# A softmax stage in which every second slot takes a whole output chunk around its transposes, and the slot between them none

## The chip, the cores and the metric

One NeuronCore of a Trainium2 chip runs the whole program. TensorE (PE, and PEld for its weight loads), VectorE (DVE), ScalarE (ACT), GpSimd (POOL) and SyncE (SP, which here only issues DMAs) each run their own list of instructions in order and wait for each other by semaphores. The metric is the time of one execution on the device, in microseconds (us), as the median of several runs.

## The reference

Two layers over a sequence of 2048 tokens with 1024 channels, float32. Layer 0 is windowed attention with a learned sink per head: 16 query heads share 4 key/value heads (4 to each), 64 channels a head, and each block of 128 queries sees its own and the previous block of keys. Layer 1 is a pooling mixer. Around each stand a modulated RMS norm, a gate and a residual.

```python
h = rms_norm(x, norm_g[i]) * (1.0 + scale) + shift
# layer 0
scores = einsum('bnqkgd,bnskd->bnkgqs', qb, kb) * HEAD_DIM ** -0.5     # then masked to the window
m = maximum(max(scores), sink)
p = exp(scores - m)
probs = p / (sum(p) + exp(sink - m))
o = einsum('bnkgqs,bnskd->bnqkgd', probs, vb)
branch = (o * silu(g)) @ w_out
x = x + gate * branch
# layer 1: pooled means over windows of 2, 4, 8, 16, a group projection, silu gate, w_out, gate, residual
```

## The kernel before

Four stages follow one another on all engines: the q, k, v projection (`qkv_stage`), the gate projection (`gate_stage`), attention with its output projection (`attend_stage`), and the whole pooling layer (`pool_stage`). All matmuls are float32 work done as three products of a high and a low part (`PRODUCTS`). The change touches `attend_stage` alone.

The stage runs over 64 units. A unit is one block of 128 queries and one key/value head with its 4 query heads. What one unit needs is spread over several slots of a loop that every engine runs over the same index i. In slot i:

- PE makes the scores of unit i (S: 8 matmuls, `scores`, line 1371), transposes the probabilities of unit i-1 (T: 4 transposes, `p_round`, line 1381), and multiplies the probabilities of unit i-2 by the values (V: 12 matmuls, 6 in the first block, `values`, line 1399).
- ACT copies the previous block's scores out of PSUM (`previous`, line 1183), rounds the gated result of unit i-3 (`z_hi`, line 1207), rounds the transposed probabilities of unit i-1 (`p_hi`, line 1198, which waits for T), takes the four exponentials of unit i (`exps`, line 1191), and the square of a finished output chunk (`square`, line 1217).
- DVE gates the attention output of unit i-3 (`gated`, line 1289, which waits for V of unit i-3), divides the probabilities of unit i-1 (`divide`, lines 1273 and 1275, for which T waits), puts the scores of unit i together and takes their maximum (lines 1265 and 1269), makes the low part of the gated result (line 1296), adds a finished output chunk to x (`residual`, line 1304), and makes the low part of the transposed probabilities (`p_lo`, line 1281).
- POOL masks the four tiles of transposed probabilities of unit i-1 (`mask`, line 1147), and adds the square of a finished chunk to a sum (`add_square`, line 1156).

Each engine's list is fixed by the order of the Python code. So in slot i+1 the division of unit i stands behind the gating of unit i-2, and that waits for V of unit i-2, the last work of PE in slot i. V of unit u also waits for the gating of unit u-1, since both use the same PSUM bank.

The output projection of the stage (O, `output`, line 1415) is 32 chunks: 4 blocks of 512 tokens by 8 blocks of 128 output channels, 24 matmuls of 512 columns each (8 steps of k by 3 products). The last 8 come after the slots. The first 24 are put into slots 19 to 66, two slots for each: chunk c has the slots `first_slot(c)`, which is always odd, and the one after it.

```python
def first_slot(c):
    return LAP * (c // KC + 1) + BEHIND + HALVES * (c % KC)
```

Each of the two slots takes 12 of the 24 matmuls, 6 between S and T and 6 between T and V. Slots 2 to 17 have other work for the same two places (`fold`, line 1432: 6 short matmuls each, with their casts on ACT and DVE). Slot 18 has nothing in either place. Slots 64 to 66 have no S, 65 and 66 no T, and 66 no V. In slots 36 and 52 PE also sums squares (line 1354, 4 matmuls of one column). After slot 66 comes `spread_first` (line 1812), which belongs to the next stage, and then the last 8 chunks with the first norm loads and weight loads of the pooling layer beside them.

The four other engines use a chunk only when both its slots are over (`chunks_ended(i)`, again always an odd slot): SP loads the weights and x of chunk c+3 and stores chunk c, DVE adds the residual, ACT squares it, POOL adds the square.

Of the kernel before, what the change touches and what calls it, by code (L numbers as in the profile page):

```python
# [25 lines left out]
def wait(eng, sem, count):  # L26
    if count > 0:
        eng.wait_ge(sem, count)
# [931 lines left out]
def attend_stage(nc, sem_of, dims, weights, qk, ga, xt_d, sinks_d, wvt, w_group, qt_d, kt_d, vs_d, sg_d, wo_d, wp_d, x1t_d, ident,  # L960
                 gate0, rstd1):

    KC, NB, KV, HEADS, HD, D, GROUPS = (dims[n] for n in ("KC", "NB", "KV", "HEADS", "HD", "D", "GROUPS"))
# [7 lines left out]
    CHUNKS = NSB * KC  # L971
    HALVES = 2
# [11 lines left out]
    def ring(name, n):  # L984
# [13 lines left out]
    keep_cur, sinks, first, half, ones, mq, neg_max, den, rden = (sb[n] for n in (  # L998
        "keep_cur", "sinks", "first", "half", "ones", "mq", "neg_max", "den", "rden"))
# [23 lines left out]
    def first_slot(c):  # L1023
        return LAP * (c // KC + 1) + BEHIND + HALVES * (c % KC)
# [4 lines left out]
    def place(m):  # L1029
        cur, prev = m % 3, (m - 1) % 3  # L1030
        return min(cur, prev), max(cur, prev), 0 if cur < prev else 1
# [315 lines left out]
    def sum_squares(pe, s):  # L1347
        pe.wait_ge(acc_done, (KC - 1) * (s + 1))
        wait(pe, mq_done, s)
        pe.wait_ge(z_done, min(LAP * (s + 2) + 2, UNITS))  # L1350
        if s == NSB - 1:
            pe.wait_ge(x1_done, CHUNKS)
        for t in range(PER):
            last = nc.tensor.matmul(st_columns(s)[:, t:t + 1], acc[:, t * P:(t + 1) * P], ones[:, :], start=True, stop=True)
        last.then_inc(st_done, 1)

    def tensor(pe, spread_first):
        def scores(u):
            m, g = u // KV, u % KV
            low, high, _ = place(m)  # L1360
            if g == 0:
                pe.wait_ge(q_loaded[m % 2], 16 * (m // 2 + 1))
                pe.wait_ge(k_loaded[m % 3], 16 * (m // 3 + 1))
                if m == 0:
                    pe.wait_ge(zero_set, 1)
            wait(pe, cur_done, u - 1)
            if u == 1:
                pe.wait_ge(ga["mod_set"], 2)
            for h in range(GROUP):
                for part in (HI, LO):  # L1370
                    last = nc.tensor.matmul(s_ps[:, u % 2, h, :, :], qt[:, m % 2, GROUP * g + h, :],  # L1371
                                            kt[:, low:high + 1:high - low, g, part, :], start=(part == HI), stop=(part == LO))
            last.then_inc(s_done, 1)

        def p_round(u):
            pe.wait_ge(prob_done, u + 1)
            wait(pe, pl_done, u)
            if u == 0:
                pe.wait_ge(ga["silu_done"], KC * NSB - 1)
            for h in range(GROUP):  # L1380
                last = nc.tensor.transpose(tr[:, h * P:(h + 1) * P], pr[:, u % 2, h, 0:P], ident[:, :])  # L1381
            last.then_inc(ptr_done, 1)

        def values(u):
            m, g = u // KV, u % KV
            if g == 0:
                pe.wait_ge(v_loaded[m % 3], 16 * (m // 3 + 1))
            pe.wait_ge(pt_done, 4 * (u + 1))
            wait(pe, z_done, u)
            if u == 0:  # L1390
                pe.wait_ge(ga["silu_done"], KC * NSB)
            parts = [(m % 3, (CUR_HI, CUR_LO))] + ([((m - 1) % 3, (PREV_HI, PREV_LO))] if m > 0 else [])
            i = 0
            for slot, kinds in parts:
                for v_part, p_part in PRODUCTS:
                    moving = pt[:, u % 2, kinds[p_part], :].rearrange("p (a b t) -> p a b t", a=2, b=2)
                    for parity in (0, 1):
                        v = vs[:, slot, g, v_part, HD - parity * HD:HD - parity * HD + 2 * HD]
                        last = nc.tensor.matmul(o_ps[:, 0:2 * P], v, moving[:, :, parity, :],  # L1399
                                                start=(i == 0), stop=(i == 6 * len(parts) - 1))  # L1400
                        i += 1
            last.then_inc(o_done, 1)

        def output(c, ks):
            s, d = c // KC, c % KC
            if ks[0] == 0:
                pe.wait_ge(w_loaded[c % 3], 16 * (c // 3 + 1))
                wait(pe, x1_done, c - 1)
                if c < 2:
                    pe.wait_ge(fold_out, FOLDS)  # L1410
            if d == 0:
                pe.wait_ge(zlo_done, LAP * (s + 1))
            for k in ks:
                for a, b in PRODUCTS:
                    last = nc.tensor.matmul(y_ps[:, c % 2, :], w[:, c % 3, a, k, :], zt[:, s % 2, b, k, :],  # L1415
                                            start=(k == 0 and (a, b) == PRODUCTS[0]),
                                            stop=(k == KC - 1 and (a, b) == PRODUCTS[-1]))
            if ks[-1] == KC - 1:
                last.then_inc(y_done, 1)

        def fold(u, h):
            f = u // PAIRS
            if h == 0:
                pe.wait_ge(wg_lo, f + 1)
                pe.wait_ge(fold_lo, u + 1)
                wait(pe, fold_out, u - 1)
                if u < 2:
                    pe.wait_ge(ga["silu_done"], KC * NSB - 2)
            i = 0
            for c in range(GC):  # L1430
                for a, m in PRODUCTS:
                    last = nc.tensor.matmul(fold_ps[:, u % 2, h].rearrange("p c n -> p (c n)"), wv[:, u % 3, a, c, h * P:(h + 1) * P],
                                            wg[:, f % 2, m, c, :], start=(i == 0), stop=(i == 3 * GC - 1))
                    i += 1
            if h == 1:
                last.then_inc(fold_done, 1)

        pe.wait_ge(consts_set, 5)
        quarter = KC // HALVES // 2
        for i in range(LAST):  # L1440
            part = [(c, (i - first_slot(c)) * 2 * quarter) for c in range(CHUNKS - KC) if 0 <= i - first_slot(c) < HALVES]
            if i < UNITS:
                scores(i)
            if 0 <= i - 2 < FOLDS:
                fold(i - 2, 0)
            for c, k in part:
                output(c, list(range(k, k + quarter)))
            if 1 <= i <= UNITS:
                p_round(i - 1)
            if 0 <= i - 2 < FOLDS:  # L1450
                fold(i - 2, 1)
            for c, k in part:
                output(c, list(range(k + quarter, k + 2 * quarter)))
            s = (i - BEHIND - 1) // LAP - 2
            if i == LAP * (s + 2) + BEHIND + 1 and s >= 0:
                sum_squares(pe, s)
            if 2 <= i <= UNITS + 1:
                values(i - 2)
        spread_first(pe)
        for c in range(CHUNKS - KC, CHUNKS):  # L1460
            output(c, list(range(KC)))
            if c == CHUNKS - KC:
                sum_squares(pe, NSB - 2)
# [7 lines left out]
    def last_rstd(pool):  # L1471
        rstd(pool, NSB - 1)

    return {"sync": sync, "gpsimd": gpsimd, "scalar": scalar, "vector": vector, "tensor": tensor, "first_load": first_load,
            "last_sum": last_sum, "last_mean": last_mean, "last_rstd": last_rstd, "chunks": CHUNKS, "units": UNITS, "s_done": s_done,
            "pt_done": pt_done, "o_done": o_done, "y_done": y_done, "ptr_done": ptr_done, "exp_done": exp_done, "cur_done": cur_done,
# [460 lines left out]
```

## Time and profile before

| | us |
|---|---|
| median of 3 runs | 1536.61 (1533.77 to 1537.57) |
| the profiled execution | 1540.15 |
| span of its trace, first to last instruction | 1538.4 |
| PE busy | 1435.4 (93% of the span) |
| DVE busy | 890.7 (58%) |
| ACT busy | 538.0 (35%) |
| POOL busy | 386.1 (25%) |
| mean granted TensorE clock | 0.987 of full speed |

The attention stage lies between about 581 us (first S) and 1009 us (last O) of the span. In the chain of work that ended last, PE holds 68% of the span; O of this stage holds 9% of it, V 5%, S 3% and T 2%. A start time in the rows below is counted from the first instruction of the span. The time of a slot is read as the distance from the start of one S to the start of the next, since the durations that the trace gives for neighbouring matmuls overlap.

### The profile page before, as it was taken

To read this page: it belongs to the slowest core of one execution; us is meant where nothing else is said; L and a number is where in the kernel's file an instruction comes from. 1 tells how busy PE (TensorE), PEld (TensorE's weight loads), DVE (VectorE), ACT (ScalarE), POOL (GpSimd) and SP (SyncE) were. 2 spreads that over 40 slices of the span, in tenths; PEclk is the share of its full clock that TensorE was granted. 3 is DMA by queue.
4 is the path that set the end of the run, shared out by engine and by line. 5 is a ranking of instruction groups with operands and counts; after the bars stand their busy time and mean duration, and the time that the engine had idled before them with its cause. 6 is when DMAs were issued, how large, how long until landed. Compare 5 with 4: busy or idle time off the path is not lost.

```text
span 1538.4 us, 20207 instructions
## 1 busy us (share of the span) xinstructions
PE 1435.4 (93%) x7240; PEld 1210.9 (79%) x7240; DVE 890.7 (58%) x1524; ACT 538.0 (35%) x1270; POOL 386.1 (25%) x551
## 2 busy tenths in 40 slices
PE   1789999999899997789999999899999999999999
PEld 1577777788678786778888888688888888888887
DVE  7766677665434446787777775535456452645522
ACT  2433344333301115775556564322222222222200
POOL 2333333312222222454555555320000000000000
PEclk9999999999989998999999999999999999999999
DMA  8644555534987686766767765941111552112142
GB/s 309 212 165 160 197 191 191 193 121 160 345 309 275 261 321 220 268 245 232 263 251 277 274 240 194 334 126 41 55 42 62 171 193 74 42 55 75 49 150 82
DMA packets 96787, 285.62 MB, mean 186 GB/s; under 512 B 10768, under 2 KB 40496, under 8 KB 87088
## 3 DMA queue, kind: packets, MB, share of 16 engines
q1 hardware_dynamic: 87760, 250.74, 45.3%
q0 software_dynamic: 8928, 33.59, 6.2%
q8 instruction: 58, 0.95, 0.2%
q14 instruction: 41, 0.34, 0.1%
HBM read 196.22 MB, written 88.08 MB: 185 GB/s over the span
## 4 chain that ended last, share of the span: by engine, by line
PE 68%; DMA 9%; DVE 9%; issue 5%; ACT 4%; POOL 3%; SPq 1%; ACTq 0%; DVEq 0%; POOLq 0%
PE po_f_ps L1843 23%; PE po_y_ps L1859 11%; PE at_y_ps L1415 9%; PE qk_proj L667 7%; PE ga_g_ps L933 6%; PE at_o_ps L1399 5%; PE at_s_ps L1371 3%; DMA ga_ada<-in_ada_w 3%; DMA values_split<-qk_late 2%; PE at_tr L1381 2%; DMA po_xn<-x_mid_t 1%; POOL qk_rq L306 1%; ACT at_pr L1191 1%; POOL qk_acc L297 1%; DMA ga_raw<-in_attn_w_gate 1%
## 5 line engine op out<-in xcount | busy, mean ns | idle before, releaser
L1843 PE MATMUL po_f_ps<-po_ht,po_w 128*128 128x512 f32 x1536 | 348.9, 389 | 0.0
L1843 PEld LDWEIGHTS po_f_ps<-po_ht,po_w 128*128 128x128 f32 x1536 | 288.1, 188 | 60.1 <-DVE po_ht L1705 0.3
L667 PE MATMUL qk_proj<-qk_w_qkv,qk_ht 128*128 128x512 f32 x1152 | 281.9, 401 | 14.2 <-DVE qk_ht L460 8.2
L667 PEld LDWEIGHTS qk_proj<-qk_w_qkv,qk_ht 128*128 128x128 f32 x1152 | 216.9, 192 | 60.9 <-DVE qk_ht L460 9.3
L1415 PE MATMUL at_y_ps<-at_zt,at_w 128*128 128x512 f32 x768 | 197.0, 398 | 6.2 <-DVE at_x L1304 6.2
L1859 PE MATMUL po_y_ps<-po_zt,po_w 128*128 128x512 f32 x768 | 174.7, 389 | 0.0
L1859 PEld LDWEIGHTS po_y_ps<-po_zt,po_w 128*128 128x128 f32 x768 | 144.1, 188 | 29.9
L1415 PEld LDWEIGHTS at_y_ps<-at_zt,at_w 128*128 128x128 f32 x768 | 137.3, 189 | 31.4 <-issue 7.4
L1692 DVE TENSOR_TENSOR po_w<-po_raw,po_w 128x1024 fp32r<-128x1024 f32 x48 | 58.8, 1225 | 129.2 <-ACT po_w L1626 129.2
L1147 POOL TENSOR_SCALAR_AFFINE_SELECT at_pt<-at_ph 128x512 fp32r<-128x512 f32 x128 | 83.6, 676 | 187.6 <-ACT at_ph L1198 187.6
L306 POOL TENSOR_TENSOR qk_rq<-qk_mq,qk_half 128x8 f32<-128x8 f32 (+1 forms) x48 | 71.2, 1484 | 189.1 <-DVE qk_mq L487 189.1
L1191 ACT ACTIVATE at_pr<-at_sc,at_neg_max 128x129 f32<-128x129 f32 x256 | 99.6, 392 | 3.9 <-DVE at_neg_max L1269 1.6
L1399 PE MATMUL at_o_ps<-at_pt,at_vs 128*128 128x256 f32 x744 | 100.2, 284 | 0.0
L1399 PEld LDWEIGHTS at_o_ps<-at_pt,at_vs 128*128 128x128 f32 x744 | 97.1, 191 | 3.8
L1626 ACT ACTIVATE po_w<-po_raw 128x1024 fp32r<-128x1024 f32 x48 | 50.5, 1053 | 108.4 <-PE po_y_ps L1859 108.4
L1551 POOL DMA_DIRECT2D po_xn<-x_mid_t x32 | 17.5, 546 | 262.0 <-DVE po_ht L1705 255.0
L1773 DVE SCALAR_TENSOR_TENSOR po_x<-po_y_ps,mod,po_x 128x512 f32<-128x512 f32 x32 | 24.0, 751 | 99.7 <-PE po_y_ps L1859 99.7
L1147 POOL TENSOR_SCALAR_AFFINE_SELECT at_pt<-at_pl 128x512 fp32r<-128x512 f32 x128 | 78.9, 639 | 0.9
L1371 PE MATMUL at_s_ps<-at_kt,at_qt 128*128 128x256 f32 x512 | 73.4, 287 | 0.0
L933 PE MATMUL ga_g_ps<-ga_x,ga_w_late 128*128 128x512 f32 x288 | 69.4, 402 | 0.0
L872 ACT ACTIVATE ga_sg<-ga_g_ps 128x512 f32<-128x512 f32 x32 | 19.0, 595 | 143.9 <-PE ga_g_ps L933 115.3
L1381 PE MATMUL at_tr<-ident,at_pr 128*128 128x128 f32 x256 | 41.4, 285 | 28.3 <-DVE at_pr L1275 28.3
(168 smaller groups left out, 2013.0 us busy)
## 6 DMA issues: line engine op xcount, KB each, us to landing
at_w<-out_weight_split SPq DMA_DIRECT2D x32, 1024.0 KB, 6.3
queries_t<-qk_late SPq DMA_DIRECT2D x16, 1024.0 KB, 4.2
ga_ada<-in_ada_w POOLq DMA_DIRECT2D x64, 256.0 KB, 4.5
at_qt<-queries_t SPq DMA_DIRECT2D x16, 1024.0 KB, 8.1
ht_split<-qk_ht SPq DMA_DIRECT2D x6, 2048.0 KB, 9.6
values_split<-qk_late SPq DMA_DIRECT2D x16, 768.0 KB, 4.9
at_vs<-values_split SPq DMA_DIRECT2D x16, 768.0 KB, 4.9
qk_late<-in_ada_w SPq DMA_DIRECT2D x16, 512.0 KB, 6.1
```

Source lines behind the costliest of these rows:

```text
L306: nc.gpsimd.tensor_tensor(rq[:, heads], mq[:, heads], half[:, heads], ALU.pow).then_inc(rq_done, 1)
L667: last = nc.tensor.matmul(proj[:, b * BANK:(b + 1) * BANK], ht[:, s % 2, m, k, t * P:(t + 1) * P], w_qkv[:, w, k, b * BANK:(b + 1) * BANK] ...
L933: last = nc.tensor.matmul(g_bank(q), split_of(f, w)[:, k * P:(k + 1) * P], h, start=(i == 0), stop=(i == 3 * KC - 1))
L1147: nc.gpsimd.affine_select(out=pt[:, u % 2, kind, :].rearrange("p (h t) -> p h t", h=GROUP), in_=(ph if hi else pl)[:, :].rearrange("p (h t ...
L1191: last = nc.scalar.activation(pr[:, u % 2, h, :], sc[:, g, h, :], ACT.Exp, bias=neg_max[:, u % 2, h:h + 1], accum_out=den[:, u % 2, h:h + 1])
L1371: last = nc.tensor.matmul(s_ps[:, u % 2, h, :, :], qt[:, m % 2, GROUP * g + h, :], kt[:, low:high + 1:high - low, g, part, :], start=(part ...
L1381: last = nc.tensor.transpose(tr[:, h * P:(h + 1) * P], pr[:, u % 2, h, 0:P], ident[:, :])
L1399: last = nc.tensor.matmul(o_ps[:, 0:2 * P], v, moving[:, :, parity, :], start=(i == 0), stop=(i == 6 * len(parts) - 1))
L1415: last = nc.tensor.matmul(y_ps[:, c % 2, :], w[:, c % 3, a, k, :], zt[:, s % 2, b, k, :], start=(k == 0 and (a, b) == PRODUCTS[0]), stop=( ...
L1692: nc.vector.tensor_tensor(w[:, i % 2, LO].rearrange("p k c -> p (k c)"), raw[:, (RING0 + i) % RAW].rearrange("p k c -> p (k c)"), w[:, i % ...
L1843: last = nc.tensor.matmul(f_ps[:, bank(j, h), :], w[:, i % 2, a, k, :], ht[:, h, m, k, :], start=(n == 0), stop=(n == 3 * KC - 1))
L1859: last = nc.tensor.matmul(y_ps[:, h, :], w[:, i % 2, a, k, :], zt[:, h, m, k, :], start=(n == 0), stop=(n == 3 * KC - 1))
```

## The change

The two slots of a chunk no longer share it. The first (odd) slot takes no O at all, and the second (even) slot takes all 24 matmuls, 12 between S and T and 12 between T and V. The wait for the chunk's weights, for the residual two chunks back and (at the first chunk of a block of tokens) for the gated results goes with it to the second slot. The number of instructions of each kind is the same, and the lists of DVE, ACT, POOL and SP are unchanged.

```diff
-        quarter = KC // HALVES // 2
+        half = KC // 2
         for i in range(LAST):
-            part = [(c, (i - first_slot(c)) * 2 * quarter) for c in range(CHUNKS - KC) if 0 <= i - first_slot(c) < HALVES]
+            part = [c for c in range(CHUNKS - KC) if i - first_slot(c) == HALVES - 1]
             if i < UNITS:
                 scores(i)
...
-            for c, k in part:
-                output(c, list(range(k, k + quarter)))
+            for c in part:
+                output(c, list(range(half)))
             if 1 <= i <= UNITS:
                 p_round(i - 1)
...
-            for c, k in part:
-                output(c, list(range(k + quarter, k + 2 * quarter)))
+            for c in part:
+                output(c, list(range(half, KC)))
```

PE's list of before at slots 19 and 20 (at_s_ps is S, at_tr is T, at_o_ps is V, at_y_ps is O):

```order
L1371 MATMUL at_s_ps<-at_kt,at_qt 128x256 x8
L1415 MATMUL at_y_ps<-at_zt,at_w 128x512 x6
L1381 MATMUL at_tr<-ident,at_pr 128x128 x4
L1415 MATMUL at_y_ps<-at_zt,at_w 128x512 x6
L1399 MATMUL at_o_ps<-at_pt,at_vs 128x256 x12
L1371 MATMUL at_s_ps<-at_kt,at_qt 128x256 x8
L1415 MATMUL at_y_ps<-at_zt,at_w 128x512 x6
L1381 MATMUL at_tr<-ident,at_pr 128x128 x4
```

Slot 20 goes on as slot 19 does. PE's list of the changed kernel from the same place, slots 19 and 20 whole:

```order
L1371 MATMUL at_s_ps<-at_kt,at_qt 128x256 x8
L1381 MATMUL at_tr<-ident,at_pr 128x128 x4
L1399 MATMUL at_o_ps<-at_pt,at_vs 128x256 x12
L1371 MATMUL at_s_ps<-at_kt,at_qt 128x256 x8
L1415 MATMUL at_y_ps<-at_zt,at_w 128x512 x12
L1381 MATMUL at_tr<-ident,at_pr 128x128 x4
L1415 MATMUL at_y_ps<-at_zt,at_w 128x512 x12
L1399 MATMUL at_o_ps<-at_pt,at_vs 128x256 x12
```

The two O pieces of the odd slot now stand in the even slot, and in the odd slot T follows S directly and V follows T directly. This pattern goes on to slot 63.

PE's list of before from slot 64 to the end of the slots (at_y_ps is O, po_bc_ps is the first work of the next stage):

```order
L1415 MATMUL at_y_ps<-at_zt,at_w 128x512 x6
L1381 MATMUL at_tr<-ident,at_pr 128x128 x4
L1415 MATMUL at_y_ps<-at_zt,at_w 128x512 x6
L1399 MATMUL at_o_ps<-at_pt,at_vs 128x256 x12
L1415 MATMUL at_y_ps<-at_zt,at_w 128x512 x12
L1399 MATMUL at_o_ps<-at_pt,at_vs 128x256 x12
L1415 MATMUL at_y_ps<-at_zt,at_w 128x512 x12
L1812 MATMUL po_bc_ps<-ident,rstd 128x128 x8
```

And the same place in the changed kernel:

```order
L1415 MATMUL at_y_ps<-at_zt,at_w 128x512 x12
L1381 MATMUL at_tr<-ident,at_pr 128x128 x4
L1415 MATMUL at_y_ps<-at_zt,at_w 128x512 x12
L1399 MATMUL at_o_ps<-at_pt,at_vs 128x256 x24
L1415 MATMUL at_y_ps<-at_zt,at_w 128x512 x24
L1812 MATMUL po_bc_ps<-ident,rstd 128x128 x8
```

The V of units 62 and 63 had 12 O between them and now stand next to each other (the row of 24).

## Rows read from the trace of the kernel before

**Rows 1.** Busy by stretch: length, PE, PEld, DVE, ACT, POOL, clock, DMA share, GB/s.

```profile
690.00:940.00 250.00, 250.00 (x1600) 221.91 (x1599) 185.97 (x332) 146.91 (x505) 134.27 (x197) 1.00 0.68 255
957.00:1010.00 53.00, 46.81 (x213) 38.11 (x212) 27.75 (x40) 17.77 (x25) 19.46 (x52) 1.00 0.84 294
```

**Rows 2.** PE in order of time, slots 39 and 40 (start, length, what).

```profile
801.29 1.12 PE L1371 MATMUL at_s_ps<-at_kt,at_qt 128*128 128x256 f32 x8
802.25 1.55 PE L1415 MATMUL at_y_ps<-at_zt,at_w 128*128 128x512 f32 x6
803.64 0.60 PE L1381 MATMUL at_tr<-ident,at_pr 128*128 128x128 f32 x4
804.00 1.63 PE L1415 MATMUL at_y_ps<-at_zt,at_w 128*128 128x512 f32 x6
805.46 1.59 PE L1399 MATMUL at_o_ps<-at_pt,at_vs 128*128 128x256 f32 x12
806.88 1.12 PE L1371 MATMUL at_s_ps<-at_kt,at_qt 128*128 128x256 f32 x8
...
809.30 0.66 PE L1381 MATMUL at_tr<-ident,at_pr 128*128 128x128 f32 x4
...
812.61 1.12 PE L1371 MATMUL at_s_ps<-at_kt,at_qt 128*128 128x256 f32 x8
```

**Rows 3.** PE in order of time, slot 18 and the start of slot 19.

```profile
683.76 1.12 PE L1371 MATMUL at_s_ps<-at_kt,at_qt 128*128 128x256 f32 x8
685.68 0.66 PE L1381 MATMUL at_tr<-ident,at_pr 128*128 128x128 f32 x4 [0.81 <-DVE at_pr L1275]
686.10 1.67 PE L1399 MATMUL at_o_ps<-at_pt,at_vs 128*128 128x256 f32 x12
687.61 1.12 PE L1371 MATMUL at_s_ps<-at_kt,at_qt 128*128 128x256 f32 x8
```

**Rows 4.** DVE in order of time, slots 18 and 19.

```profile
683.96 0.43 DVE L1289 SCALAR_TENSOR_TENSOR at_z<-at_o_ps,at_sg 128x256 f32<-128x256 f32 x1 [0.53 <-PE at_o_ps L1399]
...
684.50 1.13 DVE L1275 TENSOR_TENSOR at_pr<-at_pr,at_rden 128x512 f32<-128x512 f32 x1
...
688.74 0.18 DVE L1273 RECIPROCAL at_rden<-at_den 128x4 f32<-128x4 f32 x1 [0.45 <-ACT at_pr L1191]
```

**Rows 5.** POOL in order of time, slots 18, 39 and 40.

```profile
683.87 1.22 POOL L1147 TENSOR_SCALAR_AFFINE_SELECT at_pt<-at_pl 128x512 fp32r<-128x512 f32 x2
...
806.22 1.23 POOL L1147 TENSOR_SCALAR_AFFINE_SELECT at_pt<-at_pl 128x512 fp32r<-128x512 f32 x2
807.41 1.29 POOL L1156 TENSOR_TENSOR at_acc<-at_acc,at_sqx 128x512 f32<-128x512 f32 x1
```

**Rows 6.** The divisions between 690 and 940 us (count, shortest/median/longest in ns).

```profile
L1275 DVE TENSOR_TENSOR at_pr<-at_pr,at_rden x44: 691/692/1620, 693.9 to 938.6; 128x512 f32<-128x512 f32 x44
```

**Rows 7.** DVE in order of time, slot 40.

```profile
807.63 1.62 DVE L1275 TENSOR_TENSOR at_pr<-at_pr,at_rden 128x512 f32<-128x512 f32 x1
```

**Rows 8.** Who waited for whom, 688 to 950 us (total us, times, longest).

```profile
PEld at_tr L1381 <- DVE at_pr L1275: 7.0, 19, 1.3
```

**Rows 9.** ACT in order of time, slot 39, first and last of its exponentials.

```profile
804.77 0.40 ACT L1191 ACTIVATE at_pr<-at_sc,at_neg_max 128x129 f32<-128x129 f32 x1
...
806.23 0.19 ACT L1191 ACTIVATION_READ_ACCUMULATOR at_pr<-at_sc,at_neg_max 128x1 f32 x1
```

**Rows 10.** PE in order of time, slots 63 and 64 and after slot 66.

```profile
937.90 1.12 PE L1371 MATMUL at_s_ps<-at_kt,at_qt 128*128 128x256 f32 x8
...
945.90 0.66 PE L1381 MATMUL at_tr<-ident,at_pr 128*128 128x128 f32 x4 [0.85 <-DVE at_pr L1275]
...
956.13 1.95 PE L1812 MATMUL po_bc_ps<-ident,rstd 128*128 128x128 f32 x16
```

**Rows 11.** Busy time by stretch, at the stage's start (granted clock: third from the end).

```profile
590.00:600.00 10.00, 8.06 (x45) 7.56 (x43) 6.25 (x12) 6.91 (x23) 4.80 (x8) 0.63 0.20 66
650.00:680.00 30.00, 23.53 (x192) 22.52 (x191) 22.53 (x44) 22.30 (x70) 13.88 (x23) 1.00 0.68 242
```

## Prediction

> **What bounds the kernel now.** I read the busy times by stretch first, then PE in order of time through a few slots, then DVE, ACT and POOL at the same places, then the list of waits. Through the slots that carry output matmuls PE has no gap at all: 250 us of 250 busy, at the full clock [rows 1]. DVE is busy for 74% of that stretch and the others less. So PE's own work sets the pace, and every moment for which PE has to wait there is lost. After the stage the pooling layer is bound by PE too, so a delay is not made good later. The only other idle time near the change is in the last 8 chunks, 53.00 less 46.81 = 6.2 us [rows 1].
>
> A slot of before, read from start to start [rows 2]: S 0.96 us, six O 1.39, T 0.36, six O 1.46, V 1.42, in sum 5.59. Without its twelve O (2.85) a slot would be 2.74 us of work. The next slot took 5.73: its division took 1.62 us [rows 7] and not 0.69 as most do [rows 6], because POOL's addition had begun 0.22 us earlier and held it up [rows 5]. T then had to wait a little: 0.13 us more in the slot. T has 19 short waits for the division in the list [rows 8], one of them in slot 64, so 18 x 0.13 = 2.3 us go to these meetings. As a check, from S of slot 19 at 687.61 [rows 3] to S of slot 63 at 937.90 [rows 10] are 250.29 us for 44 slots; 44 slots of 5.60 are 246.4, and the 3.9 left hold the 2.3 and the sums of squares in slots 36 and 52, which stay as they are.
>
> **The light slot (odd, no O).** This is where the change costs. T needs the division, the division stands behind the gating on DVE, and the gating needs V, which is the last thing PE did in the slot before. In before the six O between S and T hide this chain. Slot 18 of before shows it bare, as it has nothing between S and T [rows 3, 4]: S starts at 683.76, gating at 683.96 (0.20 after it), division at 684.50 (0.74 after it), it takes 1.13, and T starts 0.05 after its end, at 685.68. PE had idled for 0.81 us. V starts 0.42 after T and the next S 1.51 after V, since behind four short transposes V starts less smoothly than behind O. The slot took 3.85 us.
>
> Of that, 0.44 is again a meeting with POOL: the mask of the low part started at 683.87 [rows 5] and stretched the division from 0.69 to 1.13. In a light slot of the changed kernel POOL is idle at that time. The masks of the unit before follow from its T, 3.74 us into the heavy slot (S 0.96, twelve O 2.78). In slot 39 T started at 803.64 and the last mask ended at 806.22 + 1.23 = 807.45 [rows 2, 5], 3.8 later; so here they end at 7.5 us, while the division comes 8.37 + 0.74 = 9.1 us after that same start. So I take 0.69: the light slot is 0.20 + 0.54 + 0.69 + 0.05 = 1.48 to T, 0.42 to V, 1.51 to the next S, together 3.41 us. Against 2.74 of bare work that is 0.67 lost. Bounds: if only the reported gap without the meeting is lost (0.81 - 0.44 = 0.37), 0.37; if the meeting with POOL comes in every light slot, 3.85 - 2.74 = 1.11. I take 0.65, close to the slot 18 row with its meeting taken out. There are 23 light slots with S and T (19, 21, ... 63): 23 x 0.65 = +15.0 us.
>
> Slot 19 costs more once. Its exponentials end late after the last casts of the folds: in before the reciprocal of that slot only starts at 688.74 [rows 4], 1.13 after S. T can then start at about 688.74 + 0.21 + 0.69 + 0.06 = 689.70, 2.09 after S in place of 1.48, and V finds its masks just ready: +0.7.
>
> **The heavy slot (even, 24 O).** Its work is S 0.96, twelve O 2.78, T 0.36, twelve O 2.85, V 1.42: 8.37, which is the 5.59 of before and the 2.78 to 2.85 moved to it. Does its T wait? Unit i+1 has its S in the light slot. In slot 39 the exponentials began 804.77 - 801.29 = 3.48 after S and ended at 806.42, 5.13 after S [rows 2, 9]; reciprocal and division follow, so the division starts about 5.4 after S of the light slot and ends by 6.1, or 6.7 behind one mask. T of the heavy slot comes at 3.41 + 3.74 = 7.15. It is ready, with 0.4 to 1.0 to spare. So the 0.13 that the meeting costs now in the even slots goes as well: -2.3 us (0, if they stay in another form). The exponentials of the heavy slot's own unit stand behind the rounding that follows its T; in slot 39 they ended at 806.42, 2.8 after T [rows 2, 9], so here 6.5 after S, and the next T is due at 8.4 + 1.5. Masks and low parts are ready long before V, 6.95 into the slot. The weights and x of a chunk are wanted one slot later than before and their loads start when they did: nothing. The first chunk of each block of tokens waits for gated results one slot later: nothing is lost, and there was no gap to win.
>
> **The end.** In slot 64 T waited 0.85 in before [rows 10], with no S to cover it. Now twelve O stand there: 3.41 + 2.78 = 6.2 after S of slot 63 against a division that ends at 6.1 to 6.7, so 0 to 0.5 is left: -0.6. V of unit 63 now directly follows V of unit 62, and they share a bank that the gating has to empty: about 0.20 + 0.43 + 0.05 = +0.7, by the gating in slot 18 [rows 4]. The results for chunk 24 are ready well within the 24 O of slot 66. The last 8 chunks and the loads beside them keep their order and their triggers, and shift as a whole: 0, with 2 us either way for how the transfers fall.
>
> **Sum.** +15.0 + 0.7 - 2.3 - 0.6 + 0.7 = +13.5 us. The profiled execution took 1540.15 (span 1538.4), so it would be 1553.7; that execution lies 3.5 above the median of 1536.61, and on the median the same sum is 1550.1. With the lower bound of the light slot the sum is 23 x 0.37 + 0.7 - 2.3 - 0.6 + 0.7 = +7.0 (1543.6), with the upper one 25.5 - 1.5 = +24.0 (1560.6).
>
> **Rivals.**
>
> *A second meeting in the heavy slot.* The division is asked for at about 5.4 after S of the light slot. By then POOL is in the masks of the low part (4.9 to 6.1) and has the addition of the square queued behind them (to 7.4). If POOL's instructions get in first both times, the division starts at 7.3 and T at 8.0 in place of 7.15: 0.85 more in some 20 heavy slots, 17 us, 1567. For it: an addition did hold a division up for 0.93 us [rows 5, 7]. Against it: the longest of 44 divisions took 1.62 us [rows 6], which is 0.69 and the rest of one addition, so none was held by two of POOL's instructions in a row. The Trainium skill ("SBUF — State Buffer", section "SBUF: two separate sides") says that a DVE operation with two SBUF inputs and a GpSimd operation take the port pair that they share as an exclusive lock for the whole instruction, whichever starts first. The trace agrees with the lock (1.62 against 0.69 us); which of two waiting instructions goes next the page does not say. By the lock alone, one meeting is hidden and my sum stands; the loss of two in a row is this rival. 8%.
>
> *The clock.* If gaps in every second slot made the granted clock fall, the price would be large: between 590 and 600 us, after the stage's start with PE half idle, it was 0.63 [rows 11]. At that clock for even a tenth of the 250 us, 25 x (1/0.63 - 1) = 15 us come on top, 1565. Against it: from 650 to 680 us PE idled for 22% of the time, a gap in every slot, at a clock of 1.00 [rows 11]; the new gaps are 0.5 in 11.8 us. The Trainium skill ("TensorE: Matmul & The Clock Gate", Part 1) has the array's clock gated by how busy the PE is, which alone would speak against gaps; this case's row with larger gaps at the full clock decides. 2%.
>
> *The other side: the last 8 chunks take the loss back.* PE waits there for residuals that stand behind norm loads and weight loads on DVE. The weights of chunk 25 are loaded when chunk 22 ends, and chunk 23 now ends later after it. If the transfers then come apart so far that all 6.2 us of idle time [rows 1] go, and the light slots cost only their lower bound, the sum is 7.0 - 6.2 = +0.8, 1537.4, not slower. It decides if the spread between chunks 22 and 23 grows by several us; by my count it grows by less than 1 us. 6%.
>
> *The gating is not what T waits for.* If the order on DVE were no limit because something ends V's wait sooner, a light slot would be 2.74 and the kernel 2 to 3 us faster from the meetings that go: 1534. Slot 18 speaks plainly against it. 2%.
>
> **How the numbers follow.** My forecast, light slots at 3.2 to 3.85 us, has 82%, and its time is 1550.1. Rivals 8, 2, 6 and 2%. About 0.3%, or 4.6 us, is what a measurement of this kernel can tell from no change. Slower by more: 82 + 8 + 2, less 2 for a light slot at its lower bound with some of the end won back = 90%. Within 0.3%: 8%. Faster: 2%. The range runs from the lower bound of the light slot, 1543.5, to its upper bound, 1561.
>
> **What would show it.** Right: S to S of 3.4 us in odd slots and 8.4 in even ones, 11.8 for the pair against 11.3; a wait of PE for the division (line 1275) of about 0.5 us in front of T in the odd slots alone; the division at 0.69 in the odd slots; no wait of T in the even ones; the gap of slot 64 smaller; a gap before V of unit 63; the last 8 chunks with about 6 us idle; the clock at 1.00. Wrong: gaps at T in even slots (the second meeting), a clock below 1, or odd slots of 2.8 us.

## Result: 11 us slower, paid in the light slots

| | before | after |
|---|---|---|
| median of 14 runs, us | 1537.05 | 1548.85 |
| ratio to before | | 1.0073 (95%: 1.0059 to 1.0087) |
| span of the trace, us | 1538.4 | 1544.8 |
| S of slot 2 to S of slot 18 | 94.03 | 93.41 |
| S of slot 19 to S of slot 63 | 250.29 | 261.16 |
| S of slot 63 to the next stage's first work (line 1812) | 18.23 | 18.73 |
| from there to the first matmul of the pooling layer (line 1843) | 53.30 | 53.18 |
| from there to the end | 528.97 | 528.97 |

The ratio says 9 to 13 us, and the three stretches from slot 19 on say 10.87 + 0.50 - 0.12 = 11.25. The spans differ by only 6.4, because the profiled execution of after happened to reach slot 19 4.85 us sooner, through instructions that are the same in both kernels (682.76 against 687.61). A change inside one stage is better read from the starts of the same instructions on either side of it than from the spans.

Busy time by stretch of the changed kernel (columns as in [rows 1]):

```profile
690.00:950.00 260.00, 251.64 (x1596) 224.17 (x1594) 180.45 (x331) 144.83 (x505) 144.31 (x196) 1.00 0.65 240
957.00:1020.00 63.00, 57.18 (x262) 46.52 (x262) 31.91 (x46) 19.51 (x28) 21.13 (x53) 1.00 0.75 264
```

By the trace's busy time PE had no gap in [rows 1]; now it idles for 8.4 us of 260, at a clock of 1.00. In the last chunks it idles for 5.8 us where it was 6.2.

PE in order of time in the changed kernel, slots 39 and 40, which answer to [rows 2]:

```profile
801.93 1.12 PE L1371 MATMUL at_s_ps<-at_kt,at_qt 128*128 128x256 f32 x8
803.42 0.66 PE L1381 MATMUL at_tr<-ident,at_pr 128*128 128x128 f32 x4 [0.37 <-DVE at_pr L1275]
803.84 1.67 PE L1399 MATMUL at_o_ps<-at_pt,at_vs 128*128 128x256 f32 x12
805.35 1.12 PE L1371 MATMUL at_s_ps<-at_kt,at_qt 128*128 128x256 f32 x8
806.31 2.92 PE L1415 MATMUL at_y_ps<-at_zt,at_w 128*128 128x512 f32 x12
809.06 0.60 PE L1381 MATMUL at_tr<-ident,at_pr 128*128 128x128 f32 x4
809.42 2.99 PE L1415 MATMUL at_y_ps<-at_zt,at_w 128*128 128x512 f32 x12
812.25 1.59 PE L1399 MATMUL at_o_ps<-at_pt,at_vs 128*128 128x256 f32 x12
813.68 1.12 PE L1371 MATMUL at_s_ps<-at_kt,at_qt 128*128 128x256 f32 x8
```

The light slot takes 3.42 us with T 1.49 after S, the heavy one 8.33, and T of the heavy slot has no gap before it. The pair takes 11.75, against 11.32 in [rows 2]. Slot 19 takes 4.10, and from slot 20 on only slots 36 and 37 and slots 52 and 53, with the sums of squares, are longer (9.23 and 3.50).

DVE of the changed kernel in the same slots, which answers to [rows 4, 6, 7]:

```profile
802.13 0.42 DVE L1289 SCALAR_TENSOR_TENSOR at_z<-at_o_ps,at_sg 128x256 f32<-128x256 f32 x1 [2.86 <-PE at_o_ps L1399]
802.48 0.17 DVE L1273 RECIPROCAL at_rden<-at_den 128x4 f32<-128x4 f32 x1
802.68 0.69 DVE L1275 TENSOR_TENSOR at_pr<-at_pr,at_rden 128x512 f32<-128x512 f32 x1
...
807.40 0.80 DVE L1275 TENSOR_TENSOR at_pr<-at_pr,at_rden 128x512 f32<-128x512 f32 x1
```

It sat idle for 2.86 us in front of the gating, and then ran gating, reciprocal and division in turn while PE waited. The exponentials that this division needs had ended at 800.09, 2 us before the gating began. The last of them on ACT:

```profile
799.90 0.19 ACT L1191 ACTIVATION_READ_ACCUMULATOR at_pr<-at_sc,at_neg_max 128x1 f32 x1
```

The division of the heavy slot met POOL, but lost only 0.11 us by it. POOL at that place:

```profile
807.02 1.67 POOL L1147 TENSOR_SCALAR_AFFINE_SELECT at_pt<-at_pl 128x512 fp32r<-128x512 f32 x2 [0.83 <-DVE at_pl L1281]
808.67 1.28 POOL L1156 TENSOR_TENSOR at_acc<-at_acc,at_sqx 128x512 f32<-128x512 f32 x1
```

The division was asked for at 807.40. By the lengths it got in between the two masks: the first took 0.64 us and the second 1.08, and their pair 1.67, where it takes 1.23 in [rows 5]. The addition came behind both.

Waits of the changed kernel between 688 and 965 us (total us, times, longest), which answer to [rows 8]:

```profile
PEld at_tr L1381 <- DVE at_pr L1275: 13.2, 23, 0.7
...
PE at_tr L1381 <- DVE at_pr L1275: 8.4, 22, 0.5
...
PE at_o_ps L1399 <- DVE at_z L1289: 0.6, 1, 0.6
```

22 gaps of PE with 8.4 us in total, 0.38 each: one to each odd slot from 21 on. A gap is counted from the end that the trace gives for S, 1.12 us after its start, though work that is ready starts 0.96 after it. So the loss is read from the starts: T comes 1.49 after S in place of 0.96, and V 0.42 after T in place of 0.36, which makes 0.59 us in each light slot. In the same way the 250.00 busy us of [rows 1] hide 18 waits of T of about 0.1 us each. The last row is V of unit 63. PE at the end of the slots in the changed kernel, which answers to [rows 10]:

```profile
943.92 1.12 PE L1371 MATMUL at_s_ps<-at_kt,at_qt 128*128 128x256 f32 x8
...
947.35 2.91 PE L1415 MATMUL at_y_ps<-at_zt,at_w 128*128 128x512 f32 x12
950.25 0.66 PE L1381 MATMUL at_tr<-ident,at_pr 128*128 128x128 f32 x4
...
953.48 1.59 PE L1399 MATMUL at_o_ps<-at_pt,at_vs 128*128 128x256 f32 x12
955.68 1.66 PE L1399 MATMUL at_o_ps<-at_pt,at_vs 128*128 128x256 f32 x12 [0.61 <-DVE at_z L1289]
957.18 5.63 PE L1415 MATMUL at_y_ps<-at_zt,at_w 128*128 128x512 f32 x24
962.65 1.95 PE L1812 MATMUL po_bc_ps<-ident,rstd 128*128 128x128 f32 x16
```

The gap of 0.85 us before the last T no longer shows, and one of 0.61 before the last V has come.

### The profile page after: what moved, and what is told of

Same layout as the page of the kernel before. It is cut to its first block, busy times and chain, and to the rows that moved or that the text cites. A ratio compares the mean times of both kernels' runs of the same rounds, so it can differ in the third digit from the quotient of the medians.

```text
span 1544.8 us, 20207 instructions
## 1 busy us (share of the span) xinstructions
PE 1436.1 (93%) x7240; PEld 1212.3 (78%) x7240; DVE 886.2 (57%) x1524; ACT 535.8 (35%) x1270; POOL 396.8 (26%) x551
## 4 chain that ended last, share of the span: by engine, by line
PE 56%; DVE 6%; DMA 4%; ACT 3%; issue 2%; POOL 0%; ACTq 0%; DVEq 0%; POOLq 0%
PE po_f_ps L1843 23%; PE po_y_ps L1859 11%; PE at_y_ps L1415 9%; PE ga_g_ps L933 5%; PE at_o_ps L1399 4%; DMA po_xn<-x_mid_t 2%; PE at_tr L1381 2%; DMA ga_ada<-in_ada_w 2%; ACT at_pr L1191 2%; PE at_s_ps L1371 1%; DVE at_pr L1275 1%; DVE at_z L1289 1%; DVE at_sc L1265 1%; DVE at_neg_max L1269 1%; DMA silu_gates_t<-ga_sg 1%
## 5 line engine op out<-in xcount | busy, mean ns | idle before, releaser
L1415 PE MATMUL at_y_ps<-at_zt,at_w 128*128 128x512 f32 x768 | 186.6, 394 | 5.8 <-DVE at_x L1304 5.8
L1415 PEld LDWEIGHTS at_y_ps<-at_zt,at_w 128*128 128x128 f32 x768 | 140.4, 188 | 34.6 <-issue 7.4
L1147 POOL TENSOR_SCALAR_AFFINE_SELECT at_pt<-at_pl 128x512 fp32r<-128x512 f32 x128 | 89.1, 719 | 18.4 <-DVE at_pl L1281 18.4
```

The costliest lines, as they stand in the source:

```text
L1147: nc.gpsimd.affine_select(out=pt[:, u % 2, kind, :].rearrange("p (h t) -> p h t", h=GROUP), in_=(ph if hi else pl)[:, :].rearrange("p (h t ...
```

## Experiments

The theory that the prediction used (A): the light slot loses what T waits for the division, since the division stands on VectorE behind the gating, which waits for the V that ended the slot before. Rivals: the change from short transposes to V is what costs (B); VectorE is full and hands the wait on to another place (C); the uneven split costs as such (D).

All stretches in one table. "Slots" is S of slot 19 to S of slot 63, "end" from there to line 1812's work, and the ratio is to the kernel before, run on the same chip (its median there was 1538.40 for e1 to e4, 1538.92 for e5 and e7 to e9, and 1537.68 for e10, e12 and e14). Slots 19, 36, 37, 52 and 53 are left out of the second column.

| kernel | odd / even slot | slots | end | median | ratio (95%) |
|---|---|---|---|---|---|
| before | 5.60 / 5.60 to 5.73 | 250.29 | 18.23 | 1537.05 | 1 |
| after | 3.42 / 8.33 | 261.16 | 18.73 | 1548.85 | 1.0073 (1.0059 to 1.0087) |
| e1 | 2.83 / 8.33 | 248.59 | 18.56 | 1535.68 | 0.9984 (0.9975 to 0.9992) |
| e2 | 5.60 / 5.60 | 248.06 | 17.16 | 1535.75 | 0.9980 (0.9971 to 0.9989) |
| e3 | 3.53 / 7.66 | 248.60 | 18.17 | 1535.91 | 0.9985 (0.9973 to 0.9996) |
| e4 | 4.80 / 6.97 | 261.51 | 17.73 | 1549.86 | 1.0082 (1.0068 to 1.0096) |
| e5 | 5.59 / 5.59 | 247.91 | 17.31 | 1533.80 | 0.9973 (0.9963 to 0.9983) |
| e7 | 5.59 / 5.60 | 248.45 | 17.16 | 1538.64 | 1.0000 (0.9989 to 1.0012) |
| e8 | 3.61 / 8.33 | 265.22 | 18.92 | 1553.86 | 1.0096 (1.0078 to 1.0113) |
| e9 | 5.60 / 5.60 to 5.74 | 250.27 | 18.26 | 1537.80 | 1.0000 (0.9990 to 1.0011) |
| e10 | 5.60 / 5.60 | 248.61 | 17.16 | 1522.77 | 0.9907 (0.9890 to 0.9924) |
| e12 | 5.60 / 5.59 | 248.46 | 17.15 | 1530.24 | 0.9951 (0.9937 to 0.9965) |
| e14 | 2.83 / 8.33 | 249.26 | 18.57 | 1532.15 | 0.9960 (0.9945 to 0.9975) |

### e1: the changed kernel, the division ahead of the gating

```diff
         for i in range(LAST + 1):
             s = (i - BEHIND - 2) // LAP - 2
+            early = i > FOLDS + 2
+            if early and 1 <= i <= UNITS:
+                divide(i - 1)
...
             if 0 <= i - BEHIND < UNITS:
                 gated(i - BEHIND)
-            if 1 <= i <= UNITS:
+            if not early and 1 <= i <= UNITS:
                 divide(i - 1)
```

> The changed kernel, but on VectorE the division of unit i-1 stands ahead of the gating of unit i-3 from slot 19 on (nothing else moves). Theory A (the loss of the light slots is T waiting for the division, because the division stands behind the gating, which waits for the V that has just ended): the gap of 0.37 us before T in odd slots goes, the light slot falls from 3.42 to 2.85 to 2.9 us, the heavy one stays at 8.33, slot 64 and 19 as before or better; 22 x 0.55 = 12 us less than the changed kernel, near 1537, level with the kernel before or up to 2 us under it. Rival B (the loss is the change from short transposes to V with its weight load in the open, and not the wait): the light slot stays above 3.3 us and the time within 2 us of the changed kernel, 1547 to 1549. Rival C (VectorE is full and only hands the wait on, to V through the later gating): a gap of about 0.5 us appears in front of V instead, time within 3 us of the changed kernel.

DVE and then PE of e1 around slot 41, in order of time (its line numbers for PE are 3 higher):

```profile
807.61 0.18 DVE L1273 RECIPROCAL at_rden<-at_den 128x4 f32<-128x4 f32 x1 [0.79 <-ACT at_pr L1191]
807.82 0.69 DVE L1275 TENSOR_TENSOR at_pr<-at_pr,at_rden 128x512 f32<-128x512 f32 x1
```

```profile
809.21 1.12 PE L1374 MATMUL at_s_ps<-at_kt,at_qt 128*128 128x256 f32 x8
810.17 0.60 PE L1384 MATMUL at_tr<-ident,at_pr 128*128 128x128 f32 x4
810.53 1.68 PE L1402 MATMUL at_o_ps<-at_pt,at_vs 128*128 128x256 f32 x12
812.04 1.12 PE L1374 MATMUL at_s_ps<-at_kt,at_qt 128*128 128x256 f32 x8
```

The division is now made during the heavy slot's V, 1.4 us before the light slot's S starts, and T follows S directly. The light slot is 2.83 us: 0.59 less than in the changed kernel. Theory A holds and the others fall: V still stands directly behind T here, takes 1.51 us as in the changed kernel, nothing waits in front of it in the slots, and the split is as uneven as it was. By the medians the order of PE that was slower is level with the kernel before under the same move (e2). By the stretches it is still 1.9 us behind it, in two places: slot 19 takes 4.11 us, and in the end T of slot 64 waits for its division and V of unit 63 for the gating.

### e2: the kernel before, the division ahead of the gating

The same edit on the kernel before.

> The kernel before with the same move on VectorE alone (division ahead of gating from slot 19 on). Theory A: the division then starts right after its exponentials, mostly before POOL's addition of the square begins, so the meetings of 1.62 us go or are hidden: all slots at 5.59 to 5.60, slot 64 without its gap of 0.85, 2 to 3 us under the kernel before, 1534. If the move hands the wait on to V (rival C), the time is that of before or up to 3 us over it.

Measured as expected: every slot at 5.59 or 5.60 (6.50 with a sum of squares), 2.2 us less in the slots and 1.1 at the end, where the gap of 0.85 is gone. The ratio says 1.7 to 4.5 us. In its profiled execution the last chunks took 54.58 us in place of 53.30; over all traces here that stretch lies between 52.4 and 56.4 with no pattern that I can see, so a single one says little, and why it varies stays open.

### e3: three O back between S and T of the light slot

```diff
-        half = KC // 2
+        STEPS = (1, 0, 3, 4)
         for i in range(LAST):
-            part = [c for c in range(CHUNKS - KC) if i - first_slot(c) == HALVES - 1]
+            place_of = [(c, 2 * (i - first_slot(c))) for c in range(CHUNKS - KC) if 0 <= i - first_slot(c) < HALVES]
...
-            for c in part:
-                output(c, list(range(half)))
+            for c, j in place_of:
+                if STEPS[j]:
+                    output(c, list(range(sum(STEPS[:j]), sum(STEPS[:j + 1]))))
```

`STEPS` gives the steps of k (3 matmuls each) before and after T, first for the odd slot and then for the even one. The place after T is changed in the same way.

> The changed kernel with one step of k (3 O matmuls, 0.70 us) put back between S and T of the light slot; the heavy one has 9 before T and 12 after. Theory A: the wait is 0.53 us in each light slot (0.37 as the trace counts its gap) and 0.70 us of work covers it whole: light slot 3.55 to 3.6, heavy 7.63, pair 11.2 to 11.3 against 11.75, so 10 to 12 us under the changed kernel, 1537 to 1539. Only slot 19 keeps some 0.4 us. Rival B (change from T to V is what costs): V still follows T directly in the light slot, so at most 2 us are won.

PE of e3 in slot 41, in order of time:

```profile
809.59 1.12 PE L1371 MATMUL at_s_ps<-at_kt,at_qt 128*128 128x256 f32 x8
810.55 0.86 PE L1415 MATMUL at_y_ps<-at_zt,at_w 128*128 128x512 f32 x3
811.25 0.60 PE L1381 MATMUL at_tr<-ident,at_pr 128*128 128x128 f32 x4
811.60 1.67 PE L1399 MATMUL at_o_ps<-at_pt,at_vs 128*128 128x256 f32 x12
813.11 1.12 PE L1371 MATMUL at_s_ps<-at_kt,at_qt 128*128 128x256 f32 x8
```

0.70 us of work cover the whole wait: T starts 1.66 after S without a gap. The light slot takes 3.53, the pair 11.19, and the time is the same as that of e1. Slot 19 keeps 0.58 us (4.11), where I had expected 0.4. So an eighth of a chunk in the right place is enough, with VectorE's order as it was.

### e4: six O back in the light slot, but after T

The same edit with `STEPS = (0, 2, 3, 3)`.

> The changed kernel with two steps of k (6 O matmuls, 1.39 us) put back into the light slot, but after T; the heavy slot has 9 and 9. Theory A: work after T covers nothing that T waits for, so the gap of 0.37 us stays; only the uneven start of V behind T goes (0.1 us in each light slot): pair 11.65 to 11.7, 1 to 3 us under the changed kernel, 1546 to 1548. Rival B: the loss goes, pair 11.2, near 1537. A rival that the even split as such matters and not the place of the cover says 5 us or more are won here too.

PE of e4 in slot 39, in order of time:

```profile
803.25 1.12 PE L1371 MATMUL at_s_ps<-at_kt,at_qt 128*128 128x256 f32 x8
804.74 0.66 PE L1381 MATMUL at_tr<-ident,at_pr 128*128 128x128 f32 x4 [0.38 <-DVE at_pr L1275]
805.16 1.64 PE L1415 MATMUL at_y_ps<-at_zt,at_w 128*128 128x512 f32 x6
806.63 1.60 PE L1399 MATMUL at_o_ps<-at_pt,at_vs 128*128 128x256 f32 x12
808.06 1.12 PE L1371 MATMUL at_s_ps<-at_kt,at_qt 128*128 128x256 f32 x8
```

The gap is the same 0.38, and the pair takes 11.77. Work behind the waiting instruction covers nothing. My expectation that 0.1 us would be won in each pair was wrong: V behind O takes 1.43 and not 1.51, but now the six O stand behind T and take 1.47 in place of 1.39. In both orders whatever follows the four transposes pays that 0.08. Rival D falls too: the split of e4 is more even than that of e3, and its slots take 12.9 us more.

### e5: POOL's addition cut short

```diff
-                nc.gpsimd.tensor_tensor(acc[:, :], acc[:, :], sqx[:, c % 2], ALU.add).then_inc(acc_done, 1)
+                nc.gpsimd.tensor_tensor(acc[:, 0:8], acc[:, 0:8], sqx[:, c % 2, 0:8], ALU.add).then_inc(acc_done, 1)
```

> The kernel before with POOL's addition of the square cut to 8 of 512 columns (the rest of the sum is left out). If the meetings of the division (1.62 us) are with this addition: all slots at 5.60 and no gap in slot 64, 2 to 3 us less between S of slot 19 and the end of the slots; the time 1 to 3 us under the kernel before, as far as the last 8 chunks stay as they are. If something else holds the division up, even slots stay at 5.70 to 5.73.

All slots at 5.59 (6.49 with a sum of squares), 2.4 us less in the slots and 0.9 at the end. The meetings of [rows 7] were with this addition, and the 2.3 us that the prediction put on them is what they cost. The whole time fell a little more than expected, by 2.6 to 5.7 us.

### e8 and e9: three more reciprocals ahead of the division, in odd slots

```diff
             dve.wait_ge(exp_done, u + 1)
+            if u % 2 == 0 and u > FOLDS + 2:
+                for r in range(3):
+                    nc.vector.reciprocal(extra[:, r, :], den[:, u % 2, :])
             nc.vector.reciprocal(rden[:, u % 2, :], den[:, u % 2, :]).then_inc(rden_done, 1)
```

> The changed kernel with three more reciprocals of 4 columns (into a spare tile) ahead of the reciprocal of each odd slot from slot 21 on, so that gating to division takes longer by 3 x 0.1 to 0.17 us. Theory A (T of the light slot waits for gating, reciprocal, division in turn): the light slot grows by exactly what the division is later, 0.3 to 0.5 us, 7 to 11 us over the changed kernel, 1556 to 1560. Rival B (the change from T to V costs, VectorE's chain is not last): less than 2 us.

> The kernel before with the same three reciprocals in the same odd slots. There T comes 2.35 us after S and the division ends at 1.43, so 0.3 to 0.5 us more stay hidden behind the six O: no change within 1 us in the odd slots. If they cost here what they cost in the changed kernel, VectorE as a whole is the bound and theory A is wrong.

DVE and then PE of e8 in a light slot, in order of time:

```profile
807.21 0.30 DVE L1276 RECIPROCAL at_extra<-at_den 128x4 f32<-128x4 f32 x3
807.42 0.15 DVE L1277 RECIPROCAL at_rden<-at_den 128x4 f32<-128x4 f32 x1
807.60 0.69 DVE L1279 TENSOR_TENSOR at_pr<-at_pr,at_rden 128x512 f32<-128x512 f32 x1
```

```profile
806.66 1.12 PE L1375 MATMUL at_s_ps<-at_kt,at_qt 128*128 128x256 f32 x8
808.35 0.66 PE L1385 MATMUL at_tr<-ident,at_pr 128*128 128x128 f32 x4 [0.56 <-DVE at_pr L1279]
...
810.28 1.12 PE L1375 MATMUL at_s_ps<-at_kt,at_qt 128*128 128x256 f32 x8
```

The three cost VectorE only 0.21 us together, where I had expected 0.3 to 0.5, so e8 stayed under the 1556 to 1560 that I had put on it. The changed kernel passed 0.19 of it on in every light slot (3.61 against 3.42, 4.06 us over the slots); the kernel before passed on nothing (250.27 against 250.29). The two times alone would not tell, since the intervals of e8 and of the changed kernel overlap; the starts do. So the same delay on VectorE is paid nearly in full in the one order and is free in the other. That is theory A in numbers; B and C both fail it.

### e7, e10, e12 and e14: is there a version that beats both

The same reading finds a larger wait in slots 2 to 17, which neither kernel touches. There the division stands behind `fold_low` (the low part of an operand of the folds) as well, which waits for a cast that ScalarE makes after the exponentials. PE's list of waits in the kernel before, 600 to 680 us:

```profile
PEld at_tr L1381 <- DVE at_pr L1275: 22.1, 14, 2.1
PE at_tr L1381 <- DVE at_pr L1275: 19.3, 14, 1.9
```

All of e7, e10, e12 and e14 have the division ahead of the gating in every slot. They differ in the place of `fold_low` and in the loads:

```diff
# e7, e10: one slot later, behind p_lo
-            if i < FOLDS:
-                fold_low(i)
+            if 1 <= i <= FOLDS:
+                fold_low(i - 1)
# e12 and, on the changed kernel, e14: the same two lines directly behind divide(i - 1)
# e10 besides, on SyncE
-            if i + 3 < FOLDS:
-                load_fold(sp, i + 3)
+            if 1 <= i and i + 2 < FOLDS:
+                load_fold(sp, i + 2)
```

> The kernel before with two moves on VectorE: the division ahead of the gating in every slot, and the low part of a fold operand (fold_low) one slot later, behind the low part of the transposed probabilities. Theory A for slots 2 to 17: T waits there 1.16 to 1.79 us a slot because the division stands behind fold_low, which waits for ScalarE's cast behind the exponentials; with both out of the way VectorE has some 4.9 to 5.1 us of work a slot and bounds it, against 94.03 us for 16 slots now (5.88 each): 12 to 15 us less in this stretch, and the 2 us of the move of the division alone: 1521 to 1526. Rival: the loads of the folds (DMA busy for 0.68 of the time there) or VectorE's queue bound these slots anyway; then 0 to 4 us are won there, 1531 to 1536.

> As e7 (fold_low one slot later behind p_lo, division first in every slot, O split as in the kernel before), and SyncE asks for the operand of fold i+2 in slot i, not of fold i+3, so that it doesn't stand in front of the stores of the folded weights until the late fold_low is done. In e7 slots without DMA trouble took 4.3 to 4.9 us, but ScalarE waited 19.8 us for those stores. If SyncE's order was the cause: 16 slots in 75 to 85 us in place of 94, 1524 to 1530. If the transfers themselves are the limit (they would need the 94 us anyway): the stretch stays at 90 or more and the time at 1533 to 1537.

> The kernel before with the division ahead of the gating in every slot and fold_low of the last unit right behind the division (1.3 us later than now, not 3 to 4). T no longer waits for fold_low: slots 2 to 17 at 5.0 to 5.3 in place of 5.88 us, 9 to 14 us less there if the loads and stores keep up, and the 2 to 3 us of the slots from 19 on: 1522 to 1529. If the transfers are the limit: 1533 to 1537 as for e10.

> The changed kernel (O whole in the even slots) with the order on VectorE of e12. Theory A: with the division off the last V's path the place of O is free, so this is level with e12 within 2 us, the light slots at 2.83 and the heavy ones at 8.33. If it lies 5 us or more over e12, the change has a cost besides the wait of T.

From S of slot 2 to S of slot 18 it is 94.03 us before, 98.56 in e7, 83.73 in e10, 89.67 in e12 and 91.04 in e14. e7 missed: the late `fold_low` held up SyncE, where the next load of the folds waits for it, and the stores of the folded weights stood behind that load. ScalarE then waited for the stores. That wait in e7 and in e10, 600 to 680 us:

```profile
ACT at_folded L1232 <- DMA value_weight_folded<-at_folded: 19.8, 5, 7.0
```

```profile
ACT at_folded L1232 <- DMA value_weight_folded<-at_folded: 5.0, 2, 2.9
```

e10 asks for each load one slot later, and SyncE waits 34.1 us for `fold_low` between 580 and 690 us in place of 50.7. It is the best version, 0.76% to 1.10% under the kernel before. e12 keeps the loads and wins half as much; 1530.2 is 1.2 us over what I had expected at worst. I had expected T to be free of `fold_low` there, but between 600 and 680 us PE still waits 15.0 us for the division (19.3 in the kernel before, 2.6 in e10), and VectorE waits 9.2 us for the exponentials in front of the reciprocal. Why those exponentials end so late stays open. e14 shows what the change costs with this order on VectorE: its slots take 0.8 us more than those of e12 and its end 1.4, in the same two places as in e1. The intervals of the two times overlap.

## Why the prediction was right

- *The bound.* PE at the full clock sets the pace of the slots. Held: in the kernels without waits of T (e1, e2, e3) a pair takes 11.16 to 11.20 us however O is spread.
- *The light slot's length.* Forecast 3.41 us, measured 3.42; gating 0.20 after S, division 0.75, T 1.49. Slot 18 with its meeting taken out was the right row, and the masks did lie elsewhere.
- *The light slot's loss.* This is the term that was mis-sized, 0.65 against 0.59. The prediction's own lengths would have given less: 3.41 and 8.37 are 11.78, only 0.60 over two slots of 5.59. I had taken 2.85 us for the twelve O out of the light slot and put back only 2.78 for them in the heavy one. The difference is the slower start behind transposes, and it stays with whatever follows T, here V. e1 shows the bare light slot at 2.83, not 2.74.
- *Slot 19.* Forecast S to T 2.09 and 0.7 us extra, measured 2.08 and 4.10 - 3.42 = 0.68. PE of the changed kernel in slot 19:

```profile
682.76 1.12 PE L1371 MATMUL at_s_ps<-at_kt,at_qt 128*128 128x256 f32 x8
684.84 0.66 PE L1381 MATMUL at_tr<-ident,at_pr 128*128 128x128 f32 x4 [0.96 <-DVE at_pr L1275]
```

- *The heavy slot.* Forecast 8.37 without a wait of T, measured 8.33 without one. The rival of a second meeting did not come: the division got between the masks, and at 0.80 us was still done 0.9 before T needed it. The 2.3 us of the meetings went, as e5 sizes them.
- *The end.* -0.6 and +0.7 forecast, from the gaps; by the starts both are larger. In the kernel before, the six O of slot 64 that precede T began here, and T came 2.40 us later [rows 10]:

```profile
943.50 1.55 PE L1415 MATMUL at_y_ps<-at_zt,at_w 128*128 128x512 f32 x6
```

Six O take 1.39, and what follows a T that waited comes 0.06 later, so the wait cost 1.07. In the changed kernel T comes 2.90 after its twelve O at 947.35, where slot 40 has 2.75 without a wait: 0.2 is left, and 0.87 came back. V of unit 63 starts 2.20 after V of unit 62 and takes 1.50, where V behind O takes 1.43 each time: +0.84. With the 0.59 of light slot 63, less 0.06 for O that stand together, that makes the 0.50 of the table.
- *The sum.* Forecast +13.5, measured +11.25 by the stretches and 11.2 by the ratio. A pair grew over its 11.18 us of work by 0.57 and not 0.65: 0.06 of this is the light slot's term, and 0.02 come from O that stand together (2.83 + 8.33 = 11.16). Over 22 pairs it makes 1.8 us; the other 0.4 are at the end (0.50 with slot 63, for 0.75) and in the last chunks (-0.12, for 0).
- *The other rivals.* The clock stayed at 1.00. The last eight chunks gave 0.12 us back and not 6.2. The chunk of slot 66 ended 9.2 us after that of slot 64 (962.65 less 953.48), where it had been 8.4, so the spread did grow by less than 1 us.

## What to carry to other kernels

Work on the pace-setting engine covers a wait only if it stands between the event that starts the chain and the instruction that waits for its end; three to six matmuls before it hid the wait, none cost 0.59 us a slot, and six behind it helped nothing. Before moving work for the sake of cover, look at what the waited-for engine has queued ahead of the awaited instruction: here one swap on VectorE was worth as much as any placing of the matmuls. A move that delays a release can delay a queue that waits on it: e7 lost on SyncE what it won on VectorE, and asking for the loads one slot later gave 14.8 us in slots 2 to 17.

## What the runs showed of the hardware that I had not expected

- Matmuls behind four transposes of 128 columns take 0.08 us more in all, whether they are twelve V (1.51 for 1.43) or six O (1.47 for 1.39).
- Reciprocals of 4 columns that don't depend on each other start some 0.07 us apart, while each takes 0.15 to 0.17 us by itself (e8).
- A VectorE product of two SBUF operands that was asked for while POOL masked two tiles in a row got in between them, by the lengths (0.80 for 0.69 us, and POOL's pair 1.67 for 1.23); one that came 0.2 us after the start of POOL's addition waited for the rest of it (1.62). In none of the 64 divisions of the changed kernel did POOL hold it for two instructions; the longest was 1.14 us.
